# Decode attention: a key tile's transposes between the two latent halves of the running tile's products

## What is computed

```python
def mla_keys(lat, kr, w_uk, k_norm):
    k_nope = jnp.einsum('...c,chd->...hd', lat, w_uk)
    k_rope = jnp.broadcast_to(kr[..., None, :], k_nope.shape[:-1] + (QK_ROPE_DIM,))
    return rmsnorm(jnp.concatenate([k_nope, k_rope], axis=-1), k_norm)
...
    def one_seq(args):
        qs, pages, ln, kn = args
        lat_all = jnp.concatenate([cache_latent[pages].reshape(PAST_LEN, KV_LORA_RANK), ln], axis=0)
        kr_all = jnp.concatenate([cache_krope[pages].reshape(PAST_LEN, QK_ROPE_DIM), kn], axis=0)
        k = mla_keys(lat_all, kr_all, w_uk, k_norm)
        sc = jnp.einsum('qhd,khd->hqk', qs, k).astype(jnp.float32) * ATTN_SCALE
        sc = jnp.where(mask[None], sc, -jnp.inf)
        p = jax.nn.softmax(sc, axis=-1).astype(lat_all.dtype)
        o_lat = jnp.einsum('hqk,kc->qhc', p, lat_all)
        return jnp.einsum('qhc,chd->qhd', o_lat, w_uv)
```

## Time and profile before

| | |
|---|---|
| time, 3 runs | 2700.72 us median, 2699.07 to 2702.4 |
| span of the profiled execution | 2702.8 us (the span is what is given of it; its time by the other clock is not) |
| TensorE busy | 2583.5 us, 96% |
| VectorE busy | 1158.7 us, 43% |
| ScalarE busy | 877.3 us, 32% |
| decode products | from 715.1 to 1255 us, 128 tiles |

### The profile page before, as it was taken

How to read it: one execution, slowest core, us unless ns; L and a number is a source line. 1 busy time by engine, 2 the same in 40 slices (tenths; PEclk the granted TensorE clock), 3 DMA queues, 4 the chain that set the end, 5 groups by cost and what they waited for, 6 DMA issues and landing times.

```text
span 2702.8 us, 47851 instructions
## 1 busy us (share of the span) xinstructions
PE 2583.5 (96%) x19078; PEld 2443.0 (90%) x19078; DVE 1158.7 (43%) x1749; ACT 877.3 (32%) x1637; POOL 5.0 (0%) x20
## 2 busy tenths in 40 slices
PE   6999999959899999998999999999999999999998
PEld 5999998745688888886999999999999999999998
DVE  5444333364444444442444433444433465444422
ACT  3222223363344444442332222322222223322211
POOL 0000000000000000000000000000000000000000
PEclk9999999967999999998999999999999999999999
DMA  3233233201011111120233323333323232233232
GB/s 110 87 93 93 86 93 106 67 8 40 23 33 40 40 40 40 40 56 1 68 88 93 92 88 87 97 88 93 93 86 95 86 89 84 79 93 91 86 92 74
DMA packets 362063, 198.66 MB, mean 74 GB/s; under 512 B 26706, under 2 KB 356642, under 8 KB 361940
## 3 DMA queue, kind: packets, MB, share of 16 engines
q1 hardware_dynamic: 361920, 196.96, 25.0%
q10 hardware_dynamic: 20, 0.04, 0.0%
HBM read 194.12 MB, written 2.87 MB: 73 GB/s over the span
## 4 chain that ended last, share of the span: by engine, by line
PE 92%; DVE 4%; ACT 3%; issue 1%; DMA 0%; POOL 0%; ACTq 0%; DVEq 0%; POOLq 0%; SPq 0%
PE ps L342 22%; PE ps L346 22%; PE ps L344 22%; PE ps L1141 15%; PE ps L1086 2%; PE ps L1144 2%; PE ps L790 1%; PE ps L791 1%; PE ps L792 1%; PE ps L1077 1%; PE ps L983 1%; PE ps L1005 1%; ACT sq L1380 1%; PE ps L1078 0%; PE ps L1004 0%
## 5 line engine op out<-in xcount | busy, mean ns | idle before, releaser
L331 DVE TENSOR_TENSOR w_lo<-raw,w_hi 128x1024 fp32r<-128x1024 f32 (+2 forms) x328 | 391.6, 1194 | 938.0 <-ACT w_hi L325 937.8
L342 PE MATMUL ps<-h_hi,w_hi 128*128 128x260 f32 x3328 | 677.2, 285 | 15.8 <-DVE h_lo L365 7.8
L346 PE MATMUL ps<-h_hi,w_lo 128*128 128x260 f32 x3328 | 674.8, 285 | 0.0
L344 PE MATMUL ps<-h_lo,w_hi 128*128 128x260 f32 x3328 | 673.6, 284 | 0.0
L325 ACT CAST w_hi<-raw 128x1024 fp32r<-128x1024 f32 (+2 forms) x328 | 336.9, 1027 | 815.4 <-PE ps L346 758.0
L342 PEld LDWEIGHTS ps<-h_hi,w_hi 128*128 128x128 f32 x3328 | 518.2, 190 | 18.6 <-issue 12.2
L346 PEld LDWEIGHTS ps<-h_hi,w_lo 128*128 128x128 f32 x3328 | 517.3, 190 | 0.0
L344 PEld LDWEIGHTS ps<-h_lo,w_hi 128*128 128x128 f32 x3328 | 515.9, 190 | 0.0
L342 PE MATMUL ps<-g_hi,w_hi 128*128 128x260 f32 x1408 | 284.2, 283 | 0.0
L344 PE MATMUL ps<-g_lo,w_hi 128*128 128x260 f32 x1408 | 283.0, 282 | 0.0
L346 PE MATMUL ps<-g_hi,w_lo 128*128 128x260 f32 x1408 | 283.0, 282 | 0.0
(11 more groups left out here) (266 smaller groups left out, 2232.6 us busy)
## 6 DMA issues: line engine op xcount, KB each, us to landing
raw<-in_w_ffn_gate SPq DMA_DIRECT2D x88, 512.0 KB, 3.8
raw<-in_w_ffn_up SPq DMA_DIRECT2D x88, 512.0 KB, 3.8
raw<-in_w_ffn_down SPq DMA_DIRECT2D x64, 512.0 KB, 3.7
cache<-in_cache_latent SPq DMA_DIRECT2D x128, 128.0 KB, 2.0
raw<-in_w_ffn_down SPq DMA_DIRECT2D x32, 384.0 KB, 3.3
raw<-in_w_conv_in SPq DMA_DIRECT2D x24, 512.0 KB, 3.7
raw<-in_w_o_attn SPq DMA_DIRECT2D x8, 512.0 KB, 3.7
cache<-in_cache_krope SPq DMA_DIRECT2D x128, 32.0 KB, 1.8
```

What stands on the lines that cost most here:

```text
L331: nc.vector.tensor_tensor(w_lo[:, un.half, 0:n], src, w_hi[:, un.half, 0:n], ALU.subtract).then_inc(unit_lo_made, 1)
L342: nc.tensor.matmul(o[b], hi, mh[:, x0 + b * HALF:x0 + (b + 1) * HALF], start=start, stop=False)
L344: nc.tensor.matmul(o[b], hi, ml[:, x0 + b * HALF:x0 + (b + 1) * HALF], start=False, stop=False)
L346: mm = nc.tensor.matmul(o[b], lo, mh[:, x0 + b * HALF:x0 + (b + 1) * HALF], start=False, stop=stop)
```

## The change

The wait block stays ahead of half 0. `keys_at` is called once for each half, and the next tile's transposes are issued between the calls. Nothing is added or removed on any engine but for that order; ScalarE, VectorE and the queues keep theirs.

```diff
                         if t == 12 and prev:
                             pe.wait_ge(oT_made, b)
+                        keys_at(s, t, g, w, b, prev, 0)
                         if not (last and s == 1 and t == PAGES - 1):
                             if t < PAGES - 1:
                                 turn(s, t + 1, g + 1, it)
                             else:
                                 turn_next(1 - s, g + 1, it if s == 0 else it + 1)
-                        keys_at(s, t, g, w, b, prev)
+                        keys_at(s, t, g, w, b, prev, 1)
                         if t == 11 and prev:
                             turn_out(b, 7)
...
-            def keys_at(s, t, g, w, b, prev):
+            def keys_at(s, t, g, w, b, prev, c):
                 first = isinstance(g, int) and g < 2
                 o = 3 * (w % 2)
-                pe.wait_ge(latl_made, g + 1)
-                pe.wait_ge(krt_made, g + 1)
...
+                if c == 0:
+                    pe.wait_ge(latl_made, g + 1)
+                    pe.wait_ge(krt_made, g + 1)
+                    if t == 0:
+                        pe.wait_ge(query_set, b + 1)
...
+                if c == KC - 1:
+                    mm.then_inc(k_made, 1)
```

More of the change, by code:

```diff
@@ new lines, in keys_at @@
+                if c == 0:
[3 more added lines that the diff above has]
+                        pe.wait_ge(query_set, b + 1)
+                    if not first:
+                        pe.wait_ge(squares_made, g if t == PAGES // 2 else g - 1)
+                        pe.wait_ge(scores_copied, g if t == PAGES // 2 else g - 1)
+                    if t == PAGES // 2 + 1 and prev:
+                        pe.wait_ge(ol_made, b)
@@ new lines, in keys_at @@
+                th, tl = latT_hi[:, t % 2, c * P:(c + 1) * P], latT_lo[:, t % 2, c * P:(c + 1) * P]
+                for q, (x, wd) in enumerate(((th, wuk_hi), (th, wuk_lo), (tl, wuk_hi))):
+                    for e, (c0, nn) in enumerate(SPAN):
+                        mm = nc.tensor.matmul(ps[:, o + e, 0:nn], x, wd[:, c, c0:c0 + nn],
+                                              start=(c == 0 and q == 0), stop=(c == KC - 1 and q == 2))
+                    if c == 0 and q == 0:
+                        nc.tensor.matmul(ps[:, o + 2, 2 * P:2 * P + H], krT[:, t % 2, :], qrb[:], start=False, stop=False)
```

## The result

The changed kernel takes 2709.97 us (median of 5, 2709.32 to 2714.27), the kernel before in the same runs 2702.06 (2699.07 to 2703.01). The ratio is 1.003, with a 95% interval of 1.0019 to 1.0041: 7.9 us or 0.3% slower. The forecast was 2710 us. It stood on the first three runs of the kernel before, with a median of 2700.72 us, and so meant 9.3 us of loss.

What follows compares the result with a forecast made beforehand. TensorE was taken as the bound (92% of the span). Terms 2.0 + 3.6 + 1.8 + 0.3 + 2.0 = 9.7 us gave a profiled span of 2712.5, 2710 us against the median 2.1 us lower; range 2702.5 to 2719.

Steps and rivals of the forecast that it cites:

- (a) The ordinary tile: Ordinary tiles: next load possible at 3.61 to 3.77 us, due at 3.68; 0.02 us each put for 99 tiles, 2 us.
- The transposes' price of 0.25 us: Any tile: transposes cost about 0.25 us wherever they stand between products of the same type.
- (b) Tile 9: Tile 9 waits for `ol`, made behind the low half; load at 4.19 us instead of 3.68, 3.6 us in 7 sequences.
- (b) Tile 4: Tile 2's root and squares come later, so tile 4's load is 0.25 us late; 1.8 us in 7 sequences.
- (b) Tile 12: Tile 12's wait for `oT`: a product instead of a transpose starts cold behind it; 0.05 us, 0.3 in all.
- (c) The boundary: Sequence boundary: no transposes left to run during the query wait; 0.34 us lost at six of seven, 2.0 us.
- every tile late: Rival: VectorE's count needs 0.2 us to free TensorE, so ordinary tiles stall too; 13 to 20 us in all; chance 0.22.
- The rule of the Trainium skill: Late weight loads lose their lead over the matmul: up to 0.12 us a tile, up to 12 us over 99 tiles.
- no change that can be told: Rival: ordinary tiles save at most 0.07 us each behind the transposes, leaving 0.8 to 5.4 us lost; chance 0.22.
- faster: Rival: idle 0.20 us ahead of the rotary product goes in 128 tiles, 24.6 us; half would give 2696; chance 0.04.

Runs made afterwards that it cites:

- the later place: Changed kernel with the next tile's transposes one part later, behind the first part of half 1; 2752.95 us, ratio 1.0186.
- the first experiment: Changed kernel, but transposes ahead of the whole tile in tiles 0, 3, 8 and 12, between the halves in the twelve others; 2699.9 us, ratio 0.9997.
- the place one part earlier: Changed kernel with the transposes one part earlier, inside half 0 behind its second part; 2708.67 us, ratio 1.0025.
- the complement: Transposes between the halves in tiles 0, 3, 8 and 12 only, elsewhere ahead of the tile as in the kernel before; 2709.58 us, ratio 1.0032.
- the short kernel before: Kernel before without the transposes' wait for krT of two tiles back, one wait less in each tile; 2702.35 us, ratio 0.9999.

## Why the prediction was right, step by step

The mechanism came out as forecast: cost in the special tiles, none in the ordinary. The size came out smaller. The decode stage grew by 6.8 us where the sum has 9.7, and the terms were off by up to 3 us each. That the median came to 2709.97 us, against 2710, is luck: the forecast's base, 2700.72 us, is 1.3 us below the median of the kernel before in the same runs, and the medians grew by 1.1 us more than the stage did.

- **(a) The ordinary tile: right in kind, 0.02 us put, -0.014 measured.** Instead of 2.0 us lost, about 1 us was gained. The chain (1.56 us) was right, as the later place shows. The unknown was whether VectorE's signal takes 0.05 or 0.21 us. In the later place it took 0.06 (874.42 to 874.48). The step's reserve of 2 us was not needed. The transposes' price of 0.25 us, from their start to the next product's, is not what a tile gains without them: distances without transposes are 3.36 us where others are 3.68, so 0.32. The sum does not use it.
- **(b) Tile 9: right.** 0.51 us a sequence forecast, 0.56 measured, 3.9 us in seven instead of 3.6. Moving `ol` took all of it away. The 0.05 us more is in the signal: the load went 0.12 us after `ol` ended (890.38 to 890.50), not 0.05.
- **(b) Tile 4: the place was right, the size was not.** 0.25 us forecast, 0.10 measured, 0.7 us in seven instead of 1.8. The step took the squares to start when the root has ended, 4.75 us behind tile 2's load; they started 4.61 us behind it (856.38 to 860.99). The changed kernel's rows show them starting 0.21 us behind the root's start, 0.10 before its end:

```profile
860.78 0.31 ACT L1196 ACTIVATE kroot<-kinv 128x128 f32<-128x128 f32 x1
860.99 1.13 ACT L1184 ACTIVATE ksq<-ps 128x384 f32<-128x384 f32 x3
...
863.36 0.42 DVE L1247 TENSOR_TENSOR latT_lo<-ps,latT_hi 128x256 fp32r<-128x256 f32 x1
...
863.83 0.47 PEld L1142 LDWEIGHTS ps<-wuk_hi,latT_hi 128*128 128x128 f32 x3
```

- **(b) Tile 12: mis-sized.** 0.05 us a sequence forecast, 0.04 measured where the program is written out, but 0.31 in the loop, 1.4 us in seven instead of 0.3. The step asked only which instruction starts cold behind the wait. It missed what TensorE's queue must do between the wait and that instruction.
- **(c) The boundary: right**, 0.34 forecast, 0.32 measured at each of six. For the seventh, at the loop's turn, the prediction had nothing gained beside the first tile's loss. It gained 0.9 us, for a reason that is not in the step: the instruction queue moved nothing in the loop's second pass, and the wait at its turn was shorter. Without that the turn would have lost about 0.3 like the others (4.38 to 4.67 between two kernels of 71 packets).
- **Not in the sum:** the first tile of all, where the transposes of tile 1 used to run while TensorE waited for the query. Step (c) names it and sets it off against the turn. It cost 0.5 us: 0.3 for the transposes, and 0.2 in the next distance, from 5.90 to 6.10 us at a granted clock of 0.50. Nor is in the sum tile 8 of the first sequence, which has no values ahead of it and waits for the squares of tile 7; the distance at t = 7 rose there from 5.14 to 5.44 us, because the transposes used to run in that wait, as at the boundary.

The rival "every tile late" is refuted by the 3.67 us of the ordinary tile and by the eleven kinds of tile that had the middle place at no cost in the first experiment. The rule of the Trainium skill ("TensorE: Matmul & The Clock Gate", Step-by-step: what each phase is for), that weight loads are pulled ahead of running matmuls, holds in the rows: the lead of 0.11 us stayed in ordinary tiles and went to nothing where the latent was late (874.48 for the load; the matmul of that load starts at 874.48 too, in the run with the later place). The rival "no change that can be told" had the saving behind the transposes; what there is of it is 0.014 us a tile, and it does not come from the restart of the stream alone, since the place one part earlier has the same restart and does not show it. The rival "faster" is refuted for this kernel by the same 3.67 us.

## What to carry to other kernels

A step that is moved later on the busy engine gives nothing where it was already hidden; it only spends cover. So list, for each tile that differs from the others, what its next wait hangs on, and count the cover that is left: here less than 0.1 us in the ordinary tile, and too little in tiles 0, 4 and 9. Waits that stand ahead of a whole tile for a resource that only a later step needs (the bank of tile 13's transposes) are worth moving down to that step: here that gave 0.3 to 0.7 us each time. And a program's length on an engine with a loop is a quantity of its own: compare the packets of the instruction queue before a microsecond at the loop's turn is put down to the order of the work.

## What the runs showed of the hardware beside this

- Code fetch at a loop's turn. TensorE runs one loop body of 32 tiles twice. The kernel before, the complement and the one with 16 waits more in each sequence show 80 packets on the instruction queue and take 5.2 to 5.6 us at the turn. All the others show 71 packets and take 4.67 to 4.70 us there (4.38 for the short kernel before). That the code is fetched again is read from these packets. Some 16 instructions more in the body moved the changed kernel from 71 to 80, some 23 fewer moved the kernel before from 80 to 71, and at nearly equal length the place of the transposes in the body's last tile went with it.
- A register instruction and four waits behind a released wait on TensorE cost 0.3 us until the next weight load (0.34 against 0.05 and 0.06 where they do not stand behind it); satisfied waits under running products cost nothing (16 in each sequence, no distance but the loop's turn changed by more than 0.01 us on average).
- At the loop's turn of the complement TensorE's weight loads stood idle for 1.87 us, and the granted clock fell to the lower level behind it (1.5 us lost). The turns of the changed kernel, of the one with 16 more waits and of the kernel before, with 1.01, 1.62 and 1.67 us of idle load, kept the full clock. Each is one execution.
